# Four more projection chunks in rounded passes, the merge work dealt out anew, and one product moved to GpSimd

## What is computed

```python
for l in range(DEPTH):
    h = rmsnorm(x, norm_mix_g[l])
    z = h @ w_in[l]
    z_a, z_b, z_c, z_dz, z_dxbc, z_ddt, z_g = split_cols(z, IN_SPLITS)
    y_a = mixer_spatial_gating(z_a, ...)
    y_b = mixer_pool(z_b, ...)
    y_c = mixer_rwkv7(z_c, ...)      # r, k, v, decay; delta-rule state over 256 steps
    y_d = mixer_ssd(z_dz, z_dxbc, z_ddt, ...)
    proj = einsum('btkc,kcd->btkd', stack([y_a, y_b, y_c, y_d]), w_branch[l])
    merged = sum(sigmoid(z_g) * proj, axis=k)
    x = x + merged @ w_out[l]
    h = rmsnorm(x, norm_ffn_g[l])
    x = x + (swiglu(h) if l % 2 == 0 else moe_swiglu(h))
```

## Time and profile before

| | |
|---|---|
| median of 3 runs | 2045.9 us (2040.14 to 2046.44) |
| the profiled execution | 2039.63 us, its span 2037.8 us |
| PE busy | 2009.9 us, 99% of the span |
| DVE, ACT, POOL busy | 1498.6, 1174.1, 54.2 us |
| granted TensorE clock | 0.998 |

### The profile page before, as it was taken

How to read it: one execution, slowest core, us unless ns; L and a number is a source line. 1 busy time by engine, 2 the same in 40 slices (tenths; PEclk the granted TensorE clock), 3 DMA queues, 4 the chain that set the end, 5 groups by cost and what they waited for, 6 DMA issues and landing times.

```text
span 2037.8 us, 31706 instructions
## 1 busy us (share of the span) xinstructions
PE 2009.9 (99%) x12826; PEld 1658.6 (81%) x12826; DVE 1498.6 (74%) x1491; ACT 1174.1 (58%) x1067; POOL 54.2 (3%) x56
## 2 busy tenths in 40 slices
PE   8999999999999999999999999999999999999998
PEld 8888989999999988889987777777777777777775
DVE  4767565665545656754868888888888889898887
ACT  4536444433334437444557777676767777677775
POOL 0200010000000020001000000000000000000000
PEclk9999999999999999999999999999999999999999
DMA  7523224555554533222559999899989999899994
GB/s 307 183 91 120 105 104 147 181 186 183 183 187 151 186 124 124 105 84 104 184 189 368 373 353 369 329 365 368 362 339 357 366 361 367 342 355 368 361 365 192
DMA packets 70790, 503.93 MB, mean 247 GB/s; under 512 B 8320, under 2 KB 8576, under 8 KB 9984
## 3 DMA queue, kind: packets, MB, share of 16 engines
q1 hardware_dynamic: 69792, 499.03, 65.1%
q10 hardware_dynamic: 864, 2.95, 0.4%
HBM read 500.90 MB, written 1.05 MB: 246 GB/s over the span
## 4 chain that ended last, share of the span: by engine, by line
PE 58%; DVE 2%; ACT 0%; issue 0%; DVEq 0%; ACTq 0%
PE g L510 37%; PE m L510 19%; PE m L1218 1%; DVE ring_low L2143 1%; PE m L781 0%; PE m L554 0%; DVE arena L2051 0%; DVE h L2465 0%; PE g L980 0%; DVE rstd L2463 0%; DVE mg_low L2179 0%; DVE rstd L2021 0%; PE m L1211 0%; DVE arena L2165 0%; DVE h L2165 0%
## 5 line engine op out<-in xcount | busy, mean ns | idle before, releaser
L2198 DVE TENSOR_TENSOR ring_low<-ring,we_high 128x2048 fp32r<-128x2048 f32 x336 | 765.3, 2289 | 122.3 <-ACT we_high L1603 121.7
L1603 ACT ACTIVATE we_high<-ring 128x2048 fp32r<-128x2048 f32 x334 | 640.8, 1919 | 269.9 <-PE g L510 170.0
L510 PE MATMUL g<-we_high,hg_high 128*96 128x512 f32 x896 | 355.8, 397 | 0.0
L510 PE MATMUL g<-ring_low,hg_high 128*96 128x512 f32 x896 | 353.0, 394 | 0.0
L510 PE MATMUL g<-we_high,hg_low 128*96 128x512 f32 x896 | 351.9, 393 | 0.0
L510 PE MATMUL g<-h_high,ring_low 128*128 128x256 f32 x1232 | 345.1, 282 | 0.0
L510 PEld LDWEIGHTS g<-h_high,ring_low 128*128 128x128 f32 x1232 | 231.3, 189 | 0.0
L510 PE MATMUL g<-h_low,w_high 128*128 128x256 f32 x720 | 200.4, 282 | 0.0
L510 PE MATMUL g<-h_high,w_high 128*128 128x256 f32 x720 | 200.2, 281 | 0.2 <-DVE ring_low L2204 0.2
L510 PEld LDWEIGHTS g<-we_high,hg_low 128*96 128x96 f32 x896 | 144.3, 161 | 63.3
L510 PEld LDWEIGHTS g<-we_high,hg_high 128*96 128x96 f32 x896 | 144.6, 161 | 58.8
(11 more groups left out here) (327 smaller groups left out, 3160.3 us busy)
## 6 DMA issues: line engine op xcount, KB each, us to landing
ring<-stream SPq DMA_DIRECT2D x472, 1024.0 KB, 4.8
sw<-sw_in SPq DMA_DIRECT2D x1, 1088.0 KB, 11.0
sw<-sw_in ACTq DMA_DIRECT2D x1, 1088.0 KB, 8.0
x<-x_in SPq DMA_DIRECT2D x4, 256.0 KB, 4.3
out<-h ACTq DMA_DIRECT2D x4, 256.0 KB, 2.9
cc<-cc_in SPq DMA_DIRECT2D x1, 816.5 KB, 12.2
rep<-rep_in SPq DMA_DIRECT2D x1, 768.0 KB, 13.4
rep<-rep_in ACTq DMA_DIRECT2D x1, 768.0 KB, 8.0
```

The lines of the kernel that those rows point to most:

```text
L510: return pe.matmul(o, a, b, start=start, stop=stop, skip_group_check=True)
L1603: A(we_high[n % 3][:, :], ring[:, slot, :], ACT.Copy).then_inc(high_ready, 1)
L2198: TT(ring_low[:, slot, :], ring[:, slot, :], we_high[n % 3][:, :], ALU.subtract).then_inc(low_ready, 1)
```

## The change

- Chunks 14, 15, 17 and 18 of each layer become rounded. Their copies lie in `scan_even` (14, 18) and `scan_odd` (15, 17), which share memory with `w_high` and with the five slots of `z_w`. So the first copies of a layer's merge halves now wait: those in slots 0 to 2 for chunk 17 to be used, those in slots 3 and 4 for chunk 18.
- A quarter of chunk 14 stands ahead of each of the four row pairs of mixer D instead of behind it.
- `SIDE` deals out 80 of the 96 quarters instead of 76, at other points. `z_lows` follows with its counts.
- The product of the receptances with their decay (`ar[..., 1, :]`, 128 x 1024) moves from DVE to POOL; PE and DVE wait for `ar_ready` where they first need it.
- The subtractions of branches 1 and 3 (`y_lows`) stand at level 0 of their chunk.

The diff, cut to its core:

```diff
+SCAN_SPLIT = (14, 15, 17, 18)
...
-SIDE = [("cw", 4), ("ss", 4), ("bo", 8), ("sr", 4), ("kt", 2)]
+SIDE = [("cw", 6), ("ss", 4), ("bo", 8), ("sr", 4), ("kt", 2)]
 for _c in range(2):
-    SIDE += [(f"s1{_c}", 1), (f"s2{_c}", 1), (f"s3{_c}", 1)]
+    SIDE += [(f"n{_c}", _c), (f"s0{_c}", 1), (f"s1{_c}", 1), (f"s2{_c}", 1), (f"s3{_c}", 1)]
     for _v in range(6):
-        SIDE += [(f"t{_v}{_c}", 1 + (_v == 0)), (f"z{_v}{_c}", 1 + (1 < _v < 5))]
+        SIDE += [(f"t{_v}{_c}", 1 + (_v == 0)), (f"z{_v}{_c}", 1 + (_v == 0 or 1 < _v < 5))]
     SIDE += [(f"U{_c}", 1), (f"O{_c}", 1)]
-SIDE += [("mu", 4), ("va", 4), ("vr", 4)]
+SIDE += [("mu", 3), ("va", 3), ("vr", 3)]
 N_OUT = DT // 2
 N_LATE = N_MERGE + N_OUT
 N_MIX = NZ + N_LATE
...
                 for i in range(4):
+                    project_quarter(l, 14, i)
                     m_free(pe, l, f"row{i}")
                     for j in range(2):
                         hd = 2 * i + j
                         last = mm(mb(f"row{i}")[:, j * T:(j + 1) * T], ident[0:H, hd:hd + 1].to_broadcast([H, P]), d_cs)
                     fill(l, f"row{i}", last)
-                    project_quarter(l, 14, i)
 
...
                 unit, half = Z_UNITS[n], part // 2
                 if part == 0:
                     g_free(pe, l, unit)
-                w = chunk(chunk0(l) + n)
+                if part == 0:
+                    pe.wait_ge(scan_low_ready, scan_chunk(l, n))
+                low = ring_low[:, (chunk0(l) + n) % RING, :].rearrange("p (b m) -> p b m", b=BLK)
+                high = scan_w(n).rearrange("p (b m) -> p b m", b=BLK)
                 for k in range(4 * (part % 2), 4 * (part % 2) + 4):
-                    last = mm(gb(unit)[:, half * T:(half + 1) * T], w[:, DT * half + k, :], h[:, k, :], k == 0, k == DT - 1)
+                    last = three(gb(unit)[:, half * T:(half + 1) * T], high[:, DT * half + k, :], low[:, DT * half + k, :],
+                                 h_high[:, k, :], h_low[k // 4][:, k % 4, :], k == 0, k == DT - 1)
                 if part == 3:
...
+                    side(f"n{c}")
...
+                    if c == 0:
+                        pe.wait_ge(S["ar_ready"], l + 1)
...
-                        if p:
-                            side(f"s{p}{c}")
+                        side(f"s{p}{c}")
...
+            def scan_high(l, n):
+
+                c = chunk0(l) + n
+                act.wait_ge(landed[c % RING], 16 * (c // RING + 1))
+                act.wait_ge(chunks_used, c - 3 if n in (15, 18) else c - 1 if n == 17 else chunk0(l))
+                A(scan_w(n), ring[:, c % RING, :], ACT.Copy).then_inc(scan_high_ready, 1)
+
...
-                evacuate(l, Z_UNITS[12:14])
+                evacuate(l, Z_UNITS[12:13])
+                scan_high(l, 15)
+                evacuate(l, Z_UNITS[13:14])
...
+                scan_high(l, 17)
                 evacuate(l, Z_UNITS[16:17])
+                scan_high(l, 18)
...
-                    side(f"s1{c}", f"s3{c}")
+                    side(f"n{c}", f"s3{c}")
...
                     half_free(act, l, m, b)
+                    if n < N_SLOTS:
+                        act.wait_ge(chunks_used, chunk0(l) + NZ - (1 if (2 * l * N_LATE + n) % N_SLOTS < 3 else 0))
                     A(half_slot(l, m, b), half_ring(ring, l, m, b), ACT.Copy).then_inc(z_high_ready, 1)
...
-                evacuate(l, Z_UNITS[10:12])
+                evacuate(l, Z_UNITS[10:11])
+                scan_high(l, 14)
+                evacuate(l, Z_UNITS[11:12])
...
+                pool.wait_ge(S["e_ready"], 4 * (l + 1))
+                pool.wait_ge(S["rk_ready"], l + 1)
+                G.tensor_tensor(ar[:, :, :, 1, :], zc[:, 0:4, 1:T + 1].rearrange("p j (c t) -> p j c t", c=NCH),
+                                e_in.rearrange("p j (c t) -> p j c t", c=NCH), ALU.mult).then_inc(S["ar_ready"], 1)
...
+            def scan_low(l, n):
+
+                dve.wait_ge(scan_high_ready, scan_chunk(l, n))
+                slot = (chunk0(l) + n) % RING
+                TT(ring_low[:, slot, :], ring[:, slot, :], scan_w(n), ALU.subtract).then_inc(scan_low_ready, 1)
+
...
                 mix(l, 0)
+                scan_low(l, 15)
...
+                    if c == 0:
+                        scan_low(l, 17)
...
                 mixer_a_out(l)
+                scan_low(l, 18)
...
                     q.step(V.tensor_copy(small[:, 16 + c:17 + c], small[:, 13 + 20 * c:14 + 20 * c]), S["v_stats"] if c else None)
+                scan_low(l, 14)
...
-                z_lows(l, 8)
+                z_lows(l, 9)
...
-                rc = r.rearrange("p j (c t) -> p j c t", c=NCH)
-                q.add(TT(ar[:, :, :, 1, :], rc, e_in.rearrange("p j (c t) -> p j c t", c=NCH), ALU.mult), v_seq)
-                z_lows(l, 12)
+                z_lows(l, 13)
...
-                z_lows(l, 13)
+                z_lows(l, 14)
...
                     z_lows(l, SIDE_AT[f"s3{c}"][1] // 2 + 2)
-                    side(f"s1{c}", f"s3{c}")
+                    side(f"n{c}", f"s3{c}")
...
-                        if (c, lv) == (0, 1):
+                        if (c, lv) == (0, 0):
                             y_lows(l, 1)
-                        if (c, lv) == (1, 2):
+                        if (c, lv) == (1, 0):
                             y_lows(l, 3)
```

More of the change, by code:

```diff
@@ L241, in trunk @@
         z_w = part("z_w", 25192, [N_SLOTS, HALF])
+        scan_odd = part("scan_odd", 26216, [CW])
+        scan_even = part("scan_even", 28264, [CW])
         zc = tiles(4096, CT, T + 1)
@@ L365, in trunk @@
         z_high_ready = sem("z_high_ready")
+        scan_high_ready = sem("scan_high_ready")
+        scan_low_ready = sem("scan_low_ready")
         z_low_ready = sem("z_low_ready")
@@ L450, in half_free, with scan_chunk, scan_w @@
                     eng.wait_ge(half_used, before * N_LATE + n + 1)
+        def scan_chunk(l, n):
+            return len(SCAN_SPLIT) * l + SCAN_SPLIT.index(n) + 1
+        def scan_w(n):
+            return (scan_even if n % 2 == 0 else scan_odd)[:, :]
         class Count:
@@ L572, in project @@
                     split = 1 <= n <= NS
+                    in_scan = n in SCAN_SPLIT
                     if n == 1:
@@ L613, in project @@
                                 o = gb((name, i))[:, j * T:(j + 1) * T]
-                                if split:
+                                if split or in_scan:
                                     last = three(o, high[:, DT * j + k, :], low[:, DT * j + k, :], h_high[:, k, :], h_low[k // 4][:, k % 4, :],
@@ L2043, in mixer_c @@
                 for c in range(NCH):
+                    if c == 0:
+                        dve.wait_ge(S["ar_ready"], l + 1)
                     for g in range(2):
```

10 lines of the change are left out of this document (7 added, 3 removed).

## The result

The changed kernel takes 2051.04 us, the median of 18 runs (2048.54 to 2053.73). The kernel before, run on the same chips, takes 2044.58 (18 runs, 2039.58 to 2048.90). The ratio is 1.0033, 95% interval 1.0023 to 1.0043: slower, by about what a measurement can tell. The forecast was 2044.8 in a range of 2034 to 2050; the time lies above it.

What follows compares the result with a forecast made beforehand. The prediction took PE, busy 99% of the span, as the bound. Its terms summed to -1.1 us against the profiled execution's 2039.6, which lies 6.3 below the median; on the median 2044.8 us, range 2034 to 2050.

Steps and rivals of the forecast that it cites:

- What four chunks cost: Chunks 14, 15, 17, 18 on PE: each rounded chunk takes 0.97 us less, in both layers, -7.8 us.
- The rival that rounding gains nothing: A rounded chunk between other work still costs 6.9 us, so 7.8 us are lost: 2052.5 us, chance 0.05.
- Waits that go: PE's waits for the first row pair's bank, drains of `n` and `t`, and the state get covered by quarters: -7.6 us.
- The receptances on POOL: Product moved to POOL: no gain at `ab_ready`, and it holds DVE's product behind `rk_ready` 0.9 us per layer, +1.8 us.
- The first halves behind chunk 18: Merge-half copies now wait for chunk 18's end, delaying mixer C's sigmoids: +0.9 us in the second layer, nothing in the first.
- A half that comes late: Point `t0`: its first half is split only after the drains of `s`; PE waits 1.1 us four times, +4.4 us.
- A sigmoid ahead of the scan's copies: Level 0, second token chunk: ACT's merge-step-4 sigmoid delays `sc_later`; PE waits 3.2 us once a layer, +6.4 us.
- Subtractions behind a product: Level 3: POOL may hold DVE's second subtraction ahead of the drain of `t`; taken as 0, bounds 0 and +4.4 us.
- its sign of being wrong towards slower: In the changed profile, subtractions of 2.3 us standing behind products would show the prediction wrong towards slower.
- The second rival (POOL holds DVE each time): The second subtraction is held as well: +4.4, so +3.3 us in all, 2049 us; chance 0.13.
- +0.8: Three quarters per layer are taken out of longer PE runs, at 1.62 us instead of 1.49 each: +0.8 us.
- the new deal covers what it was dealt for: The late sigmoid and half don't hold PE, as DVE or ACT may be ahead: about 2036 us, chance 0.32.

Runs made afterwards that it cites:

- The run with the eighth: Changed kernel, but behind `cum_ready` VectorE splits merge halves up to the eighth, as before the change, not the ninth: 2045.52 us, ratio 1.0014 to the kernel before.
- six edits of a few lines: Changed kernel with four repairs of issue order, receptances back on VectorE, and at level 0 of the second token chunk `t` drained before the subtractions: 2026.74 us, ratio 0.9914.
- the delayed one: Kernel before the change, with nine idle copies ahead of the real `sc_later` in the second token chunk of both layers: 2055.17 us, ratio 1.0049.
- the repaired kernel with the receptances on VectorE: Changed kernel with halves to the eighth, `t0`'s half earlier, sigmoid behind level-0 copies, `t` drained before level-3 subtractions, receptances on VectorE: 2027.20 us, ratio 0.9926.

## Why the prediction was wrong

The mechanism of most terms was right, and still the sum was not: -1.1 forecast, about +5 measured at equal clock, +6.5 in the medians. Two steps failed. The wait for `rk_ready` was left as it was, and grew by 3.3 us. And of the subtractions behind a product the second was taken to keep its place, 0, where it costs 4.2. The clock came on top, some 3 us in the means, and stood in no term.

- **What four chunks cost** (-7.8). Right: 4.2 us for the four of the first layer, so -8.4. The rival that rounding gains nothing is out: rounding alone gives 5.1 at equal clock with 4.3 us of new waits against it.
- **Waits that go** (-7.6). All of them went. But one sentence of this part failed: "The other two, L2039 and L2011, keep the quarters that they had ahead of them." L2039 did. L2011, the wait for `rk_ready`, does not hang on PE's quarters alone: VectorE's count of halves ahead of it rose by one, and the ninth copy stands behind a sigmoid with its table load. 2 x 2.4 us now (L2066) against 1.5 in the earlier trace rows: **+3.3, of which the sum had nothing**. The run with the eighth, without any wait for `rk_ready`, shows it.
- **The receptances on POOL** (+1.8). POOL's product ran from 180.33 for 2.18 us, not for 2.5, and the product of DVE behind it 1.80 us instead of the forecast 2.1. It cost PE 0.74 in one layer, and in the other as much where the low clock did not lie over it. Undone: 0.2 us. Right in kind, over-sized by 0.3 to 1.1.
- **The first halves behind chunk 18** (+0.9). The 0.9 us of L1458 in the second layer: right.
- **A half that comes late** (+4.4). Four of 0.89: 3.6.
- **A sigmoid ahead of the scan's copies** (+6.4). 6.5 measured, 3.2 and 3.3. The wait came out right to a tenth, and the pieces of its chain to 0.2 (`sc_later` done 9.7 us after the last pair began), but the sum took it by itself. Behind it lay 1.9 us of another wait, and ahead of the next work a fall of the clock.
- **Subtractions behind a product** (0, bound +4.4). The bound was the truth: four waits of 1.05. "DVE starts the next operation before the last one has ended, so it may keep its place; I take 0": it does not keep it, and the second subtraction takes 2.32 us, the 2.3 that the forecast had named as its sign of being wrong towards slower. The second rival (POOL holds DVE each time) was this case, at 0.13; its 3.3 us for the whole and 2049 were 2 us short. The rule of the Trainium skill (SBUF — State Buffer, Who interferes with whom), that such instructions exclude each other whichever starts first, agrees with the three places that the traces show: 3.95 us for two subtractions, 5.09 for three, 1.80 for one product.
- **The clock**, in no term. In the profiled execution the three stretches at waits cost 1.55, 1.7 and 2.6 us by their rows at either level (as 4.36 for 3.0), the router 4.1. Of the 1.7 one microsecond lay over the wait for the half behind the receptances, which would have been waited instead. Over all runs the mean clock went from 0.996 to 0.994, some 3 us. The forecast took 2039.6 and 2045 of before as scatter; it goes with the clock, and the changed kernel has the lower end no more: the fastest run of the changed kernel is 2048.5.

With the terms at what they measured (-8.4, -7.6, +0.8, +3.3, +0.7, +0.9, +3.6, +6.5, +4.2; the +0.8 is the forecast's own) the sum is +4.0. The profiled executions differ by 13.6, of which 1.55 + 1.7 + 2.6 + 4.1 = 10.0 go to the clock: 3.6. The straight line says 5.4 at equal clock. The 2 us between these two are not settled, and nor is what the router's last part costs either kernel in the mean, since each was traced once; that before happened to show it at full clock and the changed kernel at its slowest is luck.

The reading "the new deal covers what it was dealt for" (the first rival, 2036) was wrong for this version, but its reasons were good: with six edits of a few lines (the receptances back among them), none of which touches the rounding or the quarters' order, the kernel stands at -0.86% and not at +0.33%. Five of the six are enough for -0.74%; the sixth, the drain of `t` at level 0, moved its wait elsewhere.

## What to carry to other kernels

Where work of one engine is counted "up to the nth" ahead of a critical step, the count is a dependence on everything that the other engine puts ahead of its nth: after a new deal, follow every such count to what now precedes it there, table loads too, and put the critical step ahead of it. Where GpSimd and VectorE both read two tiles of SBUF, price each long pair as one after the other, for the second and third operation as for the first, and let VectorE do first what is waited for. When a step is put ahead of others, look at who waits for those: the drain of `t` at level 0 moved the wait to branch 3. And a gap on TensorE of 2 to 4 us may not be paid by its length alone: read the granted clock around it, and compare kernels at equal clock as well as by medians.

## What the runs showed of the hardware

- At gaps of 3.2 to 4.2 us ahead of level 0 the granted clock fell to its lower level in eleven of twelve cases, in six traces. It fell between 1.2 us ahead of the gap's end and 1.3 behind it, and stayed low for 3.4 to 6.8 us, in which a matmul of 256 columns took 0.41 us instead of 0.28.
- It need not fall. In the run with the receptances back on VectorE it did not in the first layer behind 3.25 us (`279.19 0.69 PE L523 MATMUL m<-arena 128*64 128x64 f32 x16 [3.25 <-ACT arena L1497]` is the row, and 279 to 286 us were granted 1.00), though it did in the second. At gaps of 2.4 us for `rk_ready` it fell in four of ten, in the changed kernel at 813 us and not at 180. What decides is open.
- Behind a gap of 1.0 us ahead of the first row pair, between small matmuls, it fell in three of eight cases: for 10 us at 104 us and for 17 at 729 in one kernel, for 3.4 at 736 us in the delayed one, and in neither layer of before and of before with rounding alone.
- It also fell where PE had no gap, as at 339 to 344 us of the repaired kernel with the receptances on VectorE (0.66 over these 5 us, PE busy throughout).
- Seven thousandths in the mean clock of a run are 11 us here (0.999 and 0.992 of before), nearly the whole spread of that kernel. Where it was low is known only for the one execution of each kernel that was traced.
